# Zero matmuls on TensorE in the waits of a four-stage decoder trunk

## The reference

```
for i in range(DEPTH):                       # DEPTH = 2, x is 256 x 2048 float32
    m = moba_mixer(h, ...) if i % 2 == 0 else retention_mixer(h, ...)
    h = layer_norm(ALPHA * h + m, ln_g[i, 0], ln_b[i, 0])
    f = conv_ffn(h, ffn_w_in[i], conv_w[i], conv_b[i], ffn_w_out[i])
    h = layer_norm(ALPHA * h + f, ln_g[i, 1], ln_b[i, 1])
```

## Time and profile before

| | us |
|---|---|
| median of 3 runs | 2647.94 |
| the runs, lowest to highest | 2647.67 to 2648.49 |
| the profiled execution | 2648.49 |
| its span, first to last instruction | 2646.7 |
| PE busy in it | 2612.0 (99%) |
| DVE busy | 1600.4 (60%) |
| ACT busy | 1257.2 (48%) |
| mean granted PE clock | 0.995 |

### The profile page before, as it was taken

One profiled execution on the slowest core, in us unless ns is written; L12 is line 12 of the kernel. 1 busy time (PEld: TensorE's weight loads), 2 busy tenths in 40 slices (PEclk: granted clock), 3 DMA queues, 4 the chain that ended last, 5 costly groups with the idle time before them and its releaser, 6 DMA issues.

```text
span 2646.7 us, 40802 instructions
## 1 busy us (share of the span) xinstructions
PE 2612.0 (99%) x14368; PEld 2266.8 (86%) x14368; DVE 1600.4 (60%) x1842; ACT 1257.2 (48%) x1387; POOL 15.2 (1%) x38
## 2 busy tenths in 40 slices
PE   8999999999999999999999999999999999999998
PEld 8999888888888888888888888888788888888886
DVE  5666657666666654475555555554666666665455
ACT  4444435565656443334444444343365656554332
POOL 0000000000000000000000000000000000000000
PEclk9999999999999999999999999999999999999999
DMA  6545564555555565655555555566455555556654
GB/s 221 175 163 171 174 223 158 191 189 188 188 188 189 204 216 192 192 177 175 169 182 177 175 177 174 178 222 197 155 188 190 186 194 183 194 190 228 196 188 148
DMA packets 136978, 493.78 MB, mean 187 GB/s; under 512 B 15056, under 2 KB 17104, under 8 KB 135888
## 3 DMA queue, kind: packets, MB, share of 16 engines
q1 hardware_dynamic: 133136, 481.49, 55.1%
q10 hardware_dynamic: 3776, 11.37, 1.2%
HBM read 490.70 MB, written 2.10 MB: 186 GB/s over the span
## 4 chain that ended last, share of the span: by engine, by line
PE 98%; DVE 1%; DMA 0%; POOL 0%; issue 0%; ACT 0%; DVEq 0%; POOLq 0%; ACTq 0%
PE acc_ab L330 12%; PE acc_cm L330 12%; PE acc_ab L272 11%; PE acc_ab L274 11%; PE acc_ab L275 11%; PE acc_ab L333 6%; PE acc_cm L333 6%; PE acc_ab L289 5%; PE acc_ab L291 5%; PE acc_ab L293 5%; PE acc_cm L272 3%; PE acc_cm L275 3%; PE acc_cm L274 3%; PE acc_cm L356 1%; PE acc_cm L460 0%; DVE h L847 0%
## 5 line engine op out<-in xcount | busy, mean ns | idle before, releaser
L727 DVE TENSOR_TENSOR w_lo<-raw,w_hi 128x1024 fp32r<-128x1024 f32 x912 | 1105.8, 1223 | 838.2 <-ACT w_hi L507 835.2
L507 ACT ACTIVATE w_hi<-raw 128x1024 fp32r<-128x1024 f32 x912 | 948.7, 1055 | 882.7 <-PE acc_ab L275 469.7
L330 PE MATMUL acc_ab<-x_parts,w_hi 128*128 128x512 f32 x1408 | 493.7, 396 | 0.0
L330 PE MATMUL acc_cm<-x_parts,w_hi 128*128 128x512 f32 x1408 | 489.1, 394 | 0.0
L333 PE MATMUL acc_ab<-x_parts,w_lo 128*128 128x256 f32 x1408 | 391.4, 278 | 0.0
L333 PE MATMUL acc_cm<-x_parts,w_lo 128*128 128x256 f32 x1408 | 390.0, 277 | 0.0
L330 PEld LDWEIGHTS acc_ab<-x_parts,w_hi 128*128 128x128 f32 x1408 | 265.5, 189 | 61.3
L330 PEld LDWEIGHTS acc_cm<-x_parts,w_hi 128*128 128x128 f32 x1408 | 264.0, 188 | 61.3
L289 PE MATMUL acc_ab<-x_parts,w_hi 128*128 128x256 f32 x1024 | 295.8, 289 | 2.1 <-DVE w_lo L727 2.1
L291 PE MATMUL acc_ab<-x_parts,w_hi 128*128 128x256 f32 x1024 | 291.6, 285 | 0.0
L293 PE MATMUL acc_ab<-x_parts,w_lo 128*128 128x256 f32 x1024 | 291.6, 285 | 0.0
(11 more groups left out here) (111 smaller groups left out, 2839.2 us busy)
## 6 DMA issues: line engine op xcount, KB each, us to landing
raw<-in_weights_dram SPq DMA_DIRECT2D x912, 512.0 KB, 4.0
ln_gain<-in_ln_g_dram ACTq DMA_DIRECT2D x4, 1024.0 KB, 7.8
ln_bias<-in_ln_b_dram ACTq DMA_DIRECT2D x4, 1024.0 KB, 11.3
h<-in_x_dram SPq DMA_DIRECT2D x4, 512.0 KB, 8.4
decay_sb<-in_decay_tab_dram ACTq DMA_DIRECT2D x1, 1024.0 KB, 6.9
out_dram<-h SPq DMA_DIRECT2D x4, 256.0 KB, 2.5
out_dram<-h ACTq DMA_DIRECT2D x3, 256.0 KB, 2.5
conv_par<-in_conv_in_dram ACTq DMA_DIRECT2D x1, 352.0 KB, 11.4
```

Source lines behind the costliest of these rows:

```text
L330: pe.matmul(acc[:, f], w_hi[:, s % RING, k, c], x_parts[:, CK * s + k].rearrange("p a n -> p (a n)"), start=s == 0 and k == 0, stop=False, ...
L507: return act.activation(o, i, ACT.Copy)
L727: dve.tensor_tensor(w_lo[:, s], raw[:, s], w_hi[:, s].bitcast(F32), ALU.subtract).then_inc(lo_ready, 1)
```

## The change

A tile of 128 x 512 zeros is kept in SBUF. POOL fills it as its first instruction of the kernel's own. In `first_product` PE multiplies this tile by its own first 128 columns, into `mid[:, 1]`, which nothing reads: 9 times in stage 0, after a wait for the zeros and ahead of the wait for the identity, and 14 times in stages 1, 2 and 3, ahead of `turn_piece(stage, 0)` and with no wait of its own. Nothing else is changed.

```diff
+IDLE = 14
+IDLE_FIRST = 9
...
+        idle_tile = sb("idle_tile", [P, COLS], F32R)
...
+            def idle_matmuls(count):
+
+                for _ in range(count):
+                    pe.matmul(mid[:, 1], idle_tile[:, 0:P], idle_tile[:], start=True, stop=True,
+                              skip_group_check=True)
+
             def first_product(stage, turn, used, wide=False):
 
                 if stage == 0:
+                    pe.wait_ge(idle_set, 1)
+                    idle_matmuls(IDLE_FIRST)
                     pe.wait_ge(ident_in_sem, 16)
+                else:
+                    idle_matmuls(IDLE)
                 turn_piece(stage, 0)
                 turn_piece(stage, 1)
...
+            pool.memset(idle_tile[:].bitcast(F32), 0.0).then_inc(idle_set, 1)
             pool.memset(neg_half[:], -0.5).then_inc(half_set, 1)
             pool.memset(eps_tile[:], EPS).then_inc(half_set, 1)
```

More of the change, by code:

```diff
@@ L226, in build_trunk @@
         half_set = sem("half_set")
+        idle_set = sem("idle_set")
         block = ctx.enter_context(nc.Block())
```

## The result

| | us |
|---|---|
| forecast, with its range | 2644.8 (2641.6 to 2648.0) |
| with the change, 6 runs | 2662.31 median (2659.96 to 2664.57) |
| before, 6 runs beside it | 2647.81 median (2647.08 to 2656.75) |
| ratio, 95% interval | 1.005 (1.0035 to 1.0064) |
| the changed kernel's profiled execution, its span | 2662.77, 2661.0 |

One of the six runs before stands alone at 2656.75, 9 us above the others. This spread turned out to be the key.

What follows compares the result with a forecast made beforehand. PE bounds the kernel, 98% of the span. Clock gain in stages 1 to 3 of 3.4 us less 0.2 to DVE, start 0, gives 3.2: from 2648.5 to 2645.3, less 0.55 for the median, 2644.8; range 2641.6 to 2648.0.

Steps and rivals of the forecast that it cites:

- The filler costs nothing in its wait: Stages 1 to 3: the 14 zero matmuls take 3.18 us, hidden in PE's wait for DVE, with 0.5 us left.
- A clock held in full gives 5.6 us: First chunks of stages 1 to 3 at full clock and earlier product starts: 5.6 us; as a rival, chance 0.25.
- held in part: Stages 1 to 3: clock held in some cases, 3.4 us less 0.2 to DVE, 3.2 us; chance 0.40.
- Held in about half of the cases: Share 0.5 assumed for stages 1 to 3: 1.87 us where the clock holds, 0.4 where not; 3.4 us.
- The rival by which the fall is only delayed: Stages 1 to 3: filler only delays the clock's fall, gain 1.0 us, time 2646.9; chance 0.28, including no effect.
- rises no later than now: In a stage whose clock still falls, it rises no later, as the product starts no later; gain 0.4 us.
- the small sum: Stages 1 to 3: if transposes do not count as PE work, 3.1 us without counted work; gain only 1.0 us.
- DVE takes back little: Later chunks of stages 1 to 3: waits for DVE's `x_lo` take back 0.2 us, between 0 and 1.7.
- The start is worth 0: Stage 0: the clock is down again when the product starts; gain 0, from -0.3 to +2.3 us.
- start slowed: Stage 0: POOL's fill gates PE, delaying the first turning; at a 4 us fill time 2649.8; chance 0.07.
- the change removes nothing from that stream: PE's stream, 98% of the span, keeps its work; gain only where PE's clock is lower than it could be.
- a time above 2653.2: Whole kernel: slower than 2653.2 needs a fill of over 7 us or something no row shows; chance 0.04.

Runs made afterwards that it cites:

- The kernels without the lottery: Kernels in pair order with against without the change: -4.1 us; kernels with two small zero matmuls a layer, with against without the zeros of stages 1 to 3: 4.0 us.
- e2: The change with its 14 zero matmuls in stages 1 to 3 but none in stage 0; its runs with both layers fast lie within 2643.9 to 2645.9.
- e4: The whole change with the tile of zeros placed behind all other SBUF tiles; of 10 runs 3 low, 7 middle.
- f2: The kernel before, with piece 7 of x turned again, unused, behind the last chunk of each FFN layer's first wide product; mean 2665.1, 17 of 20 layers slow.
- h2: The change plus two 32-column zero matmuls in the last chunk of each FFN layer's first wide product; median 2644.03, ratio 0.9945 to the kernel before.
- i1: h2 with no zero matmuls ahead of any product; median 2648.32, ratio 0.9973 to the kernel before.
- i2: h2 with the 14 zero matmuls in stages 1 to 3 but none in stage 0; median 2644.51, ratio 0.9952 to the kernel before.
- f1: The change unchanged, ten more runs: 8 middle (2650.8 to 2653.7), 2 high (2660.3, 2661.1).

## Why the prediction was wrong, step by step

- **The filler costs nothing in its wait:** right. 14 in 3.33 us with the last one's own length, 0.36 us before DVE's signal, and the turning no later.
- **A clock held in full gives 5.6 us, and the forecast 3.2 (held in part):** right in mechanism, and in size within 1 us. The kernels without the lottery give 4.1 (2.6 to 5.6) and 4.0 (3.2 to 4.8). "Held in about half of the cases" was low: it was 19 of 27. The five runs of e2 and e4 with both layers fast gave 2643.9 to 2645.9, around the forecast's 2644.8, and the first comparison's 2662.3 less 17.8 for two slow layers is 2644.5. That it lies 0.3 from the forecast is in part luck, since two terms, the share of held stages and the gain of a stage that falls, were off in opposite directions. The rival by which the fall is only delayed, 1.0 us, is refuted as a rule and true of 8 stages of 27. In the changed kernel's profile stages 2 and 3 were held from the filler's end to the product, in stage 2 from 1151.85 (1148.52 + 3.33) to 1154.83, with only the two turnings in that stretch. In stage 1 the clock fell with the same filler and turnings, and what decides stays open. For a stage that falls I had 0.4 us, since the clock "rises no later than now". This was wrong: it rose at 411.5 in stage 1, and at 410.4 before, and the stage gained nothing. The Trainium skill says in "TensorE: Matmul & The Clock Gate", Part 4 (PE-mode transpose), that transposes do not count as a busy PE in the same way; the stages here, 19 held and 8 not with the same two turnings behind the filler, neither confirm nor refute that rule, but the small sum that I had drawn from it does not follow.
- **DVE takes back little:** right, no wait of PE for `x_lo` or `w_lo` appears in stages 1 to 3.
- **The start is worth 0:** right, 0.4 (-0.5 to 1.4). The clock had fallen again when the product ran, as said. The fill took 0.52 us where 0.6 was taken, so the rival "start slowed" has no ground.
- **The step that failed stands in the first paragraph of the prediction:** "the change removes nothing from that stream. It can gain only where PE works at a lower clock than it could." I took the 5632 wide matmuls, whose code is untouched, for a constant. They have two rhythms, 346.7 and 353.3 ns a pair, and which of them a layer's loops keep is settled by how the first product leaves off: f2, h2, i1 and i2 moved it from there. The wide stream stood in the sum with no change, and the rhythm of the two layers is worth 17.8 us, more than every term that the sum had. Why there are two rhythms, no run shows. One program has both in one execution (f1), and its levels change from run to run, so the code and the place of its tiles alone do not choose.
- **Why I did not see it.** I read only the mean in the page (394 and 277 ns), which says nothing until another profile stands beside it (399 and 281 with the change), and the three runs, all of which had drawn the fast one twice. For a time above 2653.2 I had a chance of 0.04, and "something that no row shows" is what came. The trace of before did have both: behind the turnings at 411.71 and 415.13 the pairs are slow, behind the last one fast. Had I asked of neighbouring chunks why 8 pairs took 2.82 us here and 2.77 in the loops, the question would have been there.
- **What the change does to the draw.** Over all its 106 runs, the kernel before had 39 low, 42 middle and 25 high: 92 of 212 layers slow, mean 2655.9. The change had in its 16 runs 0, 8 and 8: 24 of 32 slow, mean 2657.1, a difference of +1.2 (-1.6 to 3.9). Taken with e2 and e4, which hold the clock too, it is 40 of 72. So the gain of 4 us seems to be given back by a worse draw, but the odds differ from group to group (before alone: 18, 9, 4 and then 4, 19, 8 of 31). Each group also ran on a chip of its own, and no run tells chip from chance. So I call this not shown. Shown is that the 14 us of the first comparison were a draw and not a cost of each execution.

## What to carry to other kernels

When an untouched loop changes its speed, look at the starts of neighbouring instructions and not at their mean length, and at every single run of both kernels: levels at equal distances are modes, and a median of three or six of them says little. Find what sets the mode, and fix it (here two matmuls of 32 columns), before you measure a change that is smaller than the distance of the levels. A filler of zeros in a wait, finished about 0.4 us ahead of the signal, cost nothing and gave 4 us here by the clock.

## What the runs showed of the hardware that was not expected

- Matmuls of 512 and 256 columns in turn, each with its own weights, run in two stable rhythms at the full clock: 4 starts in 693 ns or 6 in 1060 ns. Neither changed by itself in the 21 blocks of 22 us behind the first, in any profile that has this order there and no matmul added in the loops.
- Four 128-column transposes behind a fast chunk were followed by a slow chunk 44 times of 44; behind a slow chunk by a fast one 48 times of 96 (chunks 0 to 6 of the first wide products, in the 13 profiles without the pair order there). A matmul of 32 columns at the end of the first product's last chunk, with one in its middle, left the loops fast in all 6 profiled layers, and 30 runs of 30 (h2, i1, i2) stayed within 1.7 us of their kernel's median.
- Two wide and two narrow in turn had one rhythm, 2786.7 ns a chunk; four and four 2806.7.
- The granted clock fell in 8 of 27 like stages with the same filler. In the changed kernel's profile it fell in the middle of busy matmuls (408.0, half a microsecond after the product began), so a fall can come after work has begun again.
- Matmuls of zeros can hold the clock: 19 stages of 27 stayed at 1.00 with them, and none of 18 without.
